# VectorE makes the rests of all split weights, and the split activations lie at the upper end of SBUF

## The reference

```python
# first block, twice
u = modulate(rmsnorm(h, g), shift, scale)
h = h + 0.5 * (1 + gate) * ((silu(u @ wg) * (u @ wu)) @ wd)             # feed-forward, 1024 -> 2816 -> 1024
h = h + (1 + gate) * (concat(retention, stick_breaking, mamba2)(u @ w_in) @ w_out)   # first mixer
h = h + 0.5 * (1 + gate) * swiglu(...)                                  # feed-forward
# a final norm with modulation; then the second block, twice
x = x + gate * (sum of three gated attention branches of (u @ w_in_2) @ w_out_2)     # second mixer
x = x + gate * swiglu(...)                                              # feed-forward
```

## Time and profile before

| | us |
|---|---|
| median of 3 runs | 2294.5 (2288.37 to 2294.53) |
| profiled execution, its own time | 2291.44 |
| span of its instructions | 2289.6 |
| TensorE matmul busy | 2086.4 |
| VectorE busy | 1612.0 |
| ScalarE busy | 1026.5 |
| GpSimd busy | 581.2 |
| mean granted clock of TensorE | 0.962 of full |

### The profile page before, as it was taken

How to read it: one execution, slowest core, us unless ns; L and a number is a source line. 1 busy time by engine, 2 the same in 40 slices (tenths; PEclk the granted TensorE clock), 3 DMA queues, 4 the chain that set the end, 5 groups by cost and what they waited for, 6 DMA issues and landing times. The chain is left out here.

```text
span 2289.6 us, 37587 instructions
## 1 busy us (share of the span) xinstructions
PE 2086.4 (91%) x15840; PEld 1980.4 (86%) x15840; DVE 1612.0 (70%) x2077; ACT 1026.5 (45%) x1532; POOL 581.2 (25%) x262
## 2 busy tenths in 40 slices
PE   0899999989999998999899988999999879999998
PEld 0899898889999998888899876778999767879998
DVE  3677887877777777777776776855777868645555
ACT  1544467344445446553444443353444443435443
POOL 0232203211111111353222342313233323222231
PEclk9999999999999999999899987999999989999999
DMA  8578665457777876654578743635687644334552
GB/s 291 188 272 271 208 222 173 169 190 270 263 252 246 277 261 210 212 166 156 190 271 270 254 148 115 186 136 193 222 275 251 202 136 143 120 110 148 196 179 105
DMA packets 290074, 466.38 MB, mean 204 GB/s; under 512 B 11376, under 2 KB 231152, under 8 KB 289392
## 3 DMA queue, kind: packets, MB, share of 16 engines
q1 hardware_dynamic: 252608, 326.00, 43.8%
q10 hardware_dynamic: 37296, 137.97, 16.5%
HBM read 462.88 MB, written 1.05 MB: 203 GB/s over the span
## 5 line engine op out<-in xcount | busy, mean ns | idle before, releaser
L602 PE MATMUL bank<-u_high,high 128*128 128x256 f32 (+1 forms) x3248 | 937.2, 289 | 55.9 <-DVE u_low L1479 46.6
L602 PE MATMUL bank<-u_low,high 128*128 128x256 f32 (+1 forms) x3248 | 921.5, 284 | 0.0
L602 PE MATMUL bank<-u_high,low 128*128 128x256 f32 (+1 forms) x3248 | 919.1, 283 | 0.0
L1436 DVE TENSOR_TENSOR low<-ring,high 128x1024 fp32r<-128x1024 f32 x416 | 692.1, 1681 | 237.7 <-ACT high L1053 209.6
L1904 POOL TENSOR_TENSOR low<-ring,high 128x1024 fp32r<-128x1024 f32 x186 | 483.0, 2598 | 1431.1 <-ACT high L1053 1305.9
L602 PEld LDWEIGHTS bank<-u_high,high 128*128 128x128 f32 (+1 forms) x3248 | 623.5, 192 | 74.2 <-issue 45.7
L1053 ACT ACTIVATE high<-ring 128x1024 fp32r<-128x1024 f32 x602 | 601.2, 1042 | 165.3 <-PE bank L602 95.9
L602 PEld LDWEIGHTS bank<-u_low,high 128*128 128x128 f32 (+1 forms) x3248 | 623.7, 192 | 3.8 <-issue 2.9
L602 PEld LDWEIGHTS bank<-u_high,low 128*128 128x128 f32 (+1 forms) x3248 | 622.9, 192 | 0.5
L602 PE MATMUL bank<-xa,high 128*128 128x256 f32 x2368 | 433.0, 283 | 6.5 <-DVE low L1436 4.8
L1416 DVE SCALAR_TENSOR_TENSOR ada_ring<-ada_ring,cond 128x1024 f32<-128x1024 f32 x256 | 369.5, 1445 | 18.8 <-DMA ada_ring<-ada 11.2
(11 more groups left out here) (169 smaller groups left out, 1832.7 us busy)
## 6 DMA issues: line engine op xcount, KB each, us to landing
ada_ring<-ada ACTq DMA_DIRECT2D x256, 512.0 KB, 4.7
ring<-w_in SPq DMA_DIRECT2D x76, 1024.0 KB, 5.8
ring<-ffn_wg SPq DMA_DIRECT2D x44, 1024.0 KB, 5.9
ring<-ffn_wu SPq DMA_DIRECT2D x44, 1024.0 KB, 7.5
ring<-ffn_wd SPq DMA_DIRECT2D x44, 1024.0 KB, 6.1
ring<-ffn_w_gate_up SPq DMA_DIRECT2D x44, 1024.0 KB, 6.0
ring<-ffn_w_down SPq DMA_DIRECT2D x22, 1024.0 KB, 5.1
ring<-w_out SPq DMA_DIRECT2D x20, 1024.0 KB, 5.1
```

Of the source, the lines that this page charges most:

```text
L602: return pe.e.matmul(out, lhs, rhs, start=start, stop=stop, skip_group_check=True)
L1436: dve.e.tensor_tensor(lo, src, hi.bitcast(F32), ALU.subtract).then_inc(*dve.done(("low", n)))
```

## The change

`by_pool` is gone. VectorE makes the rest of every grain, and the splitting functions and calls of `pool_program` are removed, so that GpSimd walks only through its mixer steps. Its order among these, and what each waits for, stay. `u_high` and `u_low` are placed at fixed addresses that end at byte 229312 of each partition, and `region` (66,688 bytes) ends where they begin; the tiles from `tmp` to `stat` move down by the 16,384 bytes that the two leave free.

```diff
+TOP = 229312
...
-        last = {f.grains[-1] for f in self.fills if f.grains}
-
-        self.by_pool = [n not in last and n % 2 == 0 for n in range(len(self.grains))]
...
-        self.u_high = self.sb("u_high", KT * T, F32R)
-        self.u_low = self.sb("u_low", KT * T, F32R)
...
-        base = self.at
-        self.region = self.sb("region", REGION)
+        self.u_high = self.sb("u_high", KT * T, F32R, TOP - 8 * KT * T)
+        self.u_low = self.sb("u_low", KT * T, F32R, TOP - 4 * KT * T)
+        base = TOP - 8 * KT * T - 4 * REGION
+        assert self.at <= base, (self.at, base)
+        self.region = self.sb("region", REGION, F32, base)
         self.xa = self.sb("xa", 16 * T, F32R, base + 4 * XA_AT)
         self.xr = self.sb("xr", 8 * T, F32R, base + 4 * XR_AT)
         self.merged = self.sb("merged", 16 * T, F32R, base)
...
         while dve.split < min(upto, len(STREAM.grains)):
             n = dve.split
             dve.split += 1
-            if STREAM.by_pool[n]:
-                continue
             src, hi, lo = m.grain_as(n)
...
 def pool_program(pool, m):
-    def split(upto):
-
-        while pool.split < min(upto, len(STREAM.grains)):
-            n = pool.split
-            pool.split += 1
-            if not STREAM.by_pool[n]:
-                continue
-            src, hi, lo = m.grain_as(n)
-            pool.wait_ge(("fill", STREAM.grains[n][0]), ("high", n))
-            if n >= GRAINS:
-                pool.wait_ge(("read", n - GRAINS))
-            pool.e.tensor_tensor(lo, src, hi.bitcast(F32), ALU.subtract).then_inc(*pool.done(("low", n)))
...
-        pair("xbc", 0)
-        side(0)
...
+        for unit in range(len(SIDE1)):
+            side(unit)
...
+        for unit in range(len(SIDE2)):
+            side(unit)
...
     for s in STAGES:
-        norm(s)
-        if s in FFN:
-            ffn(s)
-        elif s[0] == "m1":
+        if s[0] == "m1":
             mixer1(s)
```

More of the change, by code:

```diff
@@ L2061, in mixer2 @@
                 .then_inc(*pool.done(("total", l, 1, d), ("added", l, i)))
[L2062 to L2069, removed]
     pool.e.memset(m.ones[:, :], 1.0).then_inc(*pool.done(("ones",)))
```

## The result

The changed kernel takes 2228.8 us, the median of four runs (2221.7 to 2241.7), beside 2294.1 us for the kernel before: a ratio of 0.973, interval [0.967, 0.978], 65 us less. In a second set of runs it took 2236.3 us (ratio 0.978 [0.975, 0.980]), 53 us less. The profiled execution took 2221.72 us around a span of 2219.9 us, 69.7 us less than before's.

The account below looks back on a forecast made before the run. TensorE was taken as the bound. Feed-forward -13, first mixers -11, second mixers -12 and the tiles' place 0 summed to -36 us: 2294.5 - 36 = 2258 us, range 2236 to 2288.

Parts of the forecast that it names:

- What bounds: Whole kernel: TensorE, busy 91% of the span, is the bound; side-engine changes win only its waits, clock and matmul pace.
- Part 1, VectorE's load: VectorE takes 186 more rests, +227 us, but regains 192 and 58 us from contention: net about -20 of 1612.
- Part 1, feed-forward: Three feed-forward stages with 22 or 23 GpSimd rests come down to 197.5 us: -13 us.
- Part 1, first mixers: The two first mixers, 219.8 and 230.4 us, lose their difference by GpSimd rests: -11 us.
- small gain: Rival: similar stages differ for other reasons, only direct waits on GpSimd's rests shrink: -12 us, 2282; chance 0.17.
- Part 1, second mixers: Two second mixers: TensorE's waits on GpSimd's rests shorten, -12 us taken; the first mixer's rate would give 31.
- The queue behind a waiting rest: VectorE's in-order queue waits for ScalarE's high halves, 0.57 us per rest in a second mixer; costed at nothing.
- slower rival: Rival: VectorE becomes the second mixers' bound, net +33 us there, +9 overall, 2303; chance 0.09.
- Part 2, the place: Moving split activations up and hidden tiles down leaves matmul pace unchanged: 0 us, bounds +30 and -11.
- Slow pace: Rival: part 1 as forecast, but activation matmuls run at the hidden tiles' pace: -6 us, 2288; chance 0.08.
- fast pace: Rival: hidden-tile matmuls run at the activations' pace, 11 us more gain: -47 us, 2247; chance 0.06.
- bound of part 1: Far end for moving the rests, with the first mixer's rate for both second mixers: -13 - 11 - 31 = -55 us.

Follow-up runs that it names:

- the rests alone: Against the kernel before, VectorE makes all rests while the tiles stay at their old places: 2242.2 us, ratio 0.979.
- taken back: Against the changed kernel, GpSimd gets back its 50 rests in the two second mixers only: 2257.7 us, ratio 0.985 to the kernel before.
- idle rests: Changed kernel, plus GpSimd subtracting a scratch tile nobody reads at its 186 old places: 2340.2 us, ratio 1.022 to the kernel before.
- place alone: Against the kernel before, only the tiles move to the top; GpSimd keeps its 186 rests: 2284.9 us, ratio 0.998.
- the map: Separate kernel of matmuls alone, all 8 x 8 pairs of weight and moving-tile starts within 256 bytes, with and without a short matmul ahead; single matmuls timed.

## Why the prediction was right, and where it failed

**What bounds.** Right. TensorE stays the bound, with every gain where it had waited or run slowly.

**Part 1, VectorE's load.** Right in kind, too small. Rests at 1.233 us and products at 1.223 are what was forecast, but VectorE's busy time came to 1541.5 us, not 1590. The step priced the contention on the rests and the products alone. The other instructions of VectorE came out 48 us shorter too, 15 us of it on the 32 additions into `mods`, while those that read a bank didn't change.

**Part 1, feed-forward.** Right: 13 forecast from the twins; the kernel with the rests alone gives 3.4 + 3.9 + 3.6 = 10.9 us on the three stages with 22 or 23 GpSimd rests, and nothing on the two with 10 or 11 (0.2 us less and 0.3 more).

**Part 1, first mixers.** Right: 11 forecast, 1.4 + 11.0 = 12.4 with the rests alone. The twins had become equal, 218.4 and 219.4 us, and with that the small gain, by which they would stay 10 us apart, fell.

**Part 1, second mixers.** This is the term that failed. The prediction took 12 us, "nearest the direct waits", and kept the first mixer's rate, 31, as the bound. The measured 21.9 lies in the middle, and 25.4 when it is taken back. The direct part was sized well, 10.5 us of idle time. The other 11.4 us are mostly matmuls at the half clock, fewer of which follow when such waits go: the prediction noted the stage's clock of 0.91 and 0.92, and gave it no price. A rate from twin stages holds the clock as well as the wait, so 31, too high as it was, was the better-built of the two bounds.

**The queue behind a waiting rest.** Right to cost it at nothing: no new wait on `sil` and both second mixers shorter. The slower rival fell with that. The kernel with idle rests came out 51 us above the kernel before by another way, the hold on VectorE.

**Part 2, the place.** The step "I take 0, since no row ties the pace to an address" failed by 6 us (place alone) in a term with bounds of +30 and -11. The earlier trace rows were read rightly as two paces of equal matmuls, and the row that tells the cause was one multiplication away: the tiles' starts modulo 256. The rule of the Trainium skill named in the prediction, that TensorE never waits on anyone, gave exactly 0. On contention no run here speaks against it, but the pace changed with the tiles' place with no other engine at work, 113.3 to 120.0 ns in the map, so a sum of 0 doesn't follow from it. "Slow pace" didn't come: the activations stayed at 117.8 ns. The fast pace came in part, as 120 became 117.8 on the 3552 hidden-tile matmuls: 3552 x 2.1 = 7.5 us, some of it given back where the activations had run at 116.7. So the forecast of -36 missed the rests' 49 us by 13, most of it the second mixers' term, and the place's 6.

**Range.** Its lower end added to the bound of part 1 (-55) only "a little of the fast pace". Both bounds together are -66, and the result was -65. Two terms that both miss on the same side are not rare enough to leave out when each has its bound in the text. The second set of runs, 2236.3 us, shows how much the verdict on the range is also one of scatter: the first set's profiled run had a last stage 8.0 us shorter than before at 113.3 ns; the second set's took 195.7. The chances hold a small slip: slow pace, the rest of the small gain and half of the slower rival add to 0.08 + 0.03 + 0.045 = 0.155 for "same", not 0.14.

## What to carry to other kernels

Where two engines exclude each other, count what the second one takes from all kinds of instructions of the first, read one by one, and not only from the kind that is moved; dropping the help can be the faster way even when the first engine is the busier. Size a removed wait by twin stages of the same kernel where there are any, or add the matmuls that run at half clock after it, as they were worth about as much as the wait here (11.4 us beside 10.5, and 10.3 beside 15.1). When a trace shows two paces for equal matmuls, compare the starts of weights and moving tile modulo 256 bytes before pricing a move at nothing, and try a shift by 32 to 128 bytes: the one by 128 was worth 18 to 26 us here, the one by 32 (2228.6 us) 0 to 8.

## What the runs showed of the hardware that was not expected

- The pace of back-to-back fp32r matmuls of 128 x 128 by 256 columns depends on the distance from the weights' start to the moving tile's within 256 bytes: 113.3 to 120.2 ns at full clock, the same for both orders of outputs (in 127 of 128 pairs of chains), with the other engines quiet. The height in memory had no part in these runs: with 12 KB between them, equal offsets gave equal paces.
- Some distances have two paces (192: 113.3 or 117.8; 32: 116.7 or 117.8; in one stage of the changed kernel also 64: 113.3 beside 117.8), and a feed-forward stage of about 1600 matmuls mostly keeps one of them. The choice between 113.3 and 117.8 is worth 6 to 7 us for a stage, that between 116.7 and 117.8 about 2. It may be the source of the 20 us over which the changed kernel's runs spread; that isn't shown, as only the profiled executions tell the pace.
- GpSimd's instructions for nobody, 509 us of them, cost the program 104 us.
